# Sigmoids through ScalarE's exponential and logarithm, and the second layer's input weights held back until the expert rows are gathered

## The reference

```
h  = rms(x) * (1 + scale1) + shift1
p  = h @ w_in                         # (640, 2304)
pq, pk, pv, hq, hf_f, hf_b, hi, hg, pft = split(p)
# forget gates, forward and backward, z = hf_f or hf_b (256 columns each)
logf = log_sigmoid(z) + log1p(lb * exp(min(-z, 80)))
k    = (1 - lb) * sigmoid(-z)         # lb is 0 in layer 0
qh   = silu(hq)                       # 256 columns
o_h  = rms(gated_linear_recurrence(qh, k, hi, logf)) * silu(hg)   # hg: 256 columns
x = x + gate1 * (concat(attention, o_h, fourier) @ w_out)
x = x + gate2 * moe(h2)               # top-1 group, top-2 expert of 16 gated MLPs
```

## Time and profile before

| | |
|---|---|
| median of 3 executions | 1805.18 us (1804.99 to 1806.71) |
| the profiled execution's own time | 1805.76 us |
| its span | 1803.9 us |
| mean granted TensorE clock | 0.943 of full speed |
| busy: PE / DVE / ACT / POOL | 88% / 38% / 20% / 18% |
| DMA, mean over the span | 175 GB/s |

### The profile page before, as it was taken

One profiled execution on the slowest core, in us unless ns is written; L12 is line 12 of the kernel. 1 busy time (PEld: TensorE's weight loads), 2 busy tenths in 40 slices (PEclk: granted clock), 3 DMA queues, 4 the chain that ended last, 5 costly groups with the idle time before them and its releaser, 6 DMA issues.

```text
span 1803.9 us, 24901 instructions
## 1 busy us (share of the span) xinstructions
PE 1592.4 (88%) x10358; PEld 1159.0 (64%) x10358; DVE 686.0 (38%) x1230; ACT 369.0 (20%) x694; POOL 316.3 (18%) x305
## 2 busy tenths in 40 slices
PE   6999989777998999999969799988779859999995
PEld 5556567655555788888645556666555458888883
DVE  1284246666115122112156722757641332112224
ACT  2221246221003100000142111642200211000002
POOL 4000159332000000000100001964300010000002
PEclk9999999889998899999979899999879969999997
DMA  9921100422013999999942111013400069999985
GB/s 267 323 52 62 56 27 1 141 69 75 18 52 134 345 367 367 365 366 345 357 164 47 47 48 61 12 36 108 118 2 0 0 244 338 370 360 370 368 305 210
DMA packets 143496, 315.69 MB, mean 175 GB/s; under 512 B 25024, under 2 KB 99192, under 8 KB 130456
## 3 DMA queue, kind: packets, MB, share of 16 engines
q1 hardware_dynamic: 120240, 241.88, 39.5%
q0 software_dynamic: 11104, 37.26, 5.4%
q10 hardware_dynamic: 12040, 34.95, 4.9%
HBM read 279.46 MB, written 34.60 MB: 174 GB/s over the span
## 4 chain that ended last, share of the span: by engine, by line
PE 75%; DVE 11%; ACT 4%; DMA 4%; POOL 3%; issue 3%; ACTq 0%; POOLq 0%; DVEq 0%
PE ps L1764 20%; PE ps L1361 19%; PE ps L1778 10%; PE ps L1405 4%; PE ps L1601 3%; ACT scr L573 3%; PE ps L1481 3%; PE ps L1748 3%; POOL scr L504 2%; DVE scr L974 2%; PE ps L1661 2%; PE ps L1541 1%; PE ps L1504 1%; DMA pT<-h_rows,slot_tok 1%; DMA scr<-y_rows,slot_i 1%
## 5 line engine op out<-in xcount | busy, mean ns | idle before, releaser
L1764 PEld LDWEIGHTS ps<-hT,ring 128*128 128x128 f32 x3200 | 370.2, 194 | 26.6 <-issue 22.0
L1764 PE MATMUL ps<-hT,ring 128*128 128x128 f32 x3200 | 371.1, 277 | 3.4 <-ACT hT L573 3.4
L1361 PE MATMUL ps<-hT,ring 128*128 128x512 f32 x960 | 269.4, 442 | 19.6 <-DVE pT L1020 12.6
L1361 PEld LDWEIGHTS ps<-hT,ring 128*128 128x128 f32 x960 | 149.7, 195 | 141.7 <-issue 128.6
L1778 PE MATMUL ps<-ring,pT 128*128 128x512 f32 x400 | 179.6, 592 | 0.0
L545 POOL DMA_INDIRECT pT<-h_rows,slot_tok x50 | 47.2, 944 | 728.6 <-PE ps L1748 430.2
L573 ACT ACTIVATE pT<-ps 128x256 f32<-128x256 f32 (+3 forms) x74 | 33.4, 457 | 685.2 <-PE ps L1764 495.0
L1316 DVE TENSOR_TENSOR pT<-ps,pT 128x256 f32<-128x256 f32 x50 | 21.3, 425 | 328.5 <-ACT pT L573 328.5
L1361 PE MATMUL ps<-pT,ring 128*128 128x512 f32 (+1 forms) x512 | 139.0, 434 | 1.7 <-ACT pT L573 1.7
L504 POOL TENSOR_SCALAR scr<-scr,st 128x640 f32<-128x640 f32 (+1 forms) x80 | 128.7, 1627 | 43.4 <-DVE st L1029 43.3
L1778 PEld LDWEIGHTS ps<-ring,pT 128*128 128x128 f32 x400 | 72.3, 190 | 72.7 <-issue 72.7
(11 more groups left out here) (228 smaller groups left out, 1864.4 us busy)
## 6 DMA issues: line engine op xcount, KB each, us to landing
ring<-in_w_gate_dram SPq DMA_DIRECT2D x50, 1024.0 KB, 7.4
ring<-in_w_up_dram SPq DMA_DIRECT2D x50, 1024.0 KB, 7.7
ring<-in_w_down_dram SPq DMA_DIRECT2D x50, 1024.0 KB, 7.0
ring<-in_w_ada_dram SPq DMA_DIRECT2D x48, 1024.0 KB, 5.7
y_rows<-pT ACTq DMA_DIRECT2D x50, 512.0 KB, 8.1
ring<-in_w_in_dram SPq DMA_DIRECT2D x14, 1024.0 KB, 11.9
h_rows<-scr ACTq DMA_DIRECT2D x10, 512.0 KB, 2.6
ring<-in_w_in_dram SPq DMA_DIRECT2D x16, 256.0 KB, 4.5
```

The source lines that it names most:

```text
L1361: ins = mm(out[:, a:b], lhs, rhs[:, a:b], start=start, stop=stop, **kw)
L1764: last = mm(bank(2 + j, P, at + c * P), w[:, k, c * P:(c + 1) * P], xk[:, j, k, :], start=(k == 0), stop=(k == KC - 1))
```

## The change

Two independent edits. **The sigmoids.** For the gates, sigmoid(-z) = en / den is now computed as exp(min(-z, 0) - ln(den)): DVE subtracts the logarithm that is there anyway (semaphore `gt_d`), ACT exponentiates in place (`gt_k`), and DVE multiplies by `omlb` after the scan. For the SiLUs, ACT computes exp(-ln(1 + exp(-z))) in three steps, each waiting for the one before, and DVE keeps the last product alone. **The weights.** SP waits for all ten gathers of layer 0 before it issues the first `in` item of layer 1; everything behind it on SP waits with it.

```diff
@@ SP
                 elif kind == "in":
+                    if l > 0 and i == 0:
+                        for t in range(TT):
+                            sp.wait_ge(y_in[t], 32 * l)
@@ ACT gate
                 if l > 0:
                     A_(scr[:, 8, :], scr[:, 9, :], ACT.Ln).then_inc(gt_ln, 1)
+                act.wait_ge(gt_d, n + 1)
+                A_(scr[:, 10, :], scr[:, 10, :], ACT.Exp).then_inc(gt_k, 1)
@@ ACT silu
-                A_(scr[:, i % 2, :], pT[:, GATE_CHUNKS[i], :], ACT.Exp, scale=-1.0).then_inc(sl_e, 1)
+                e = scr[:, i % 2, :]
+                seq(A_(e, pT[:, GATE_CHUNKS[i], :], ACT.Exp, scale=-1.0))
+                seq(A_(e, e, ACT.Ln, bias=ones[:, 0:1]))
+                A_(e, e, ACT.Exp, scale=-1.0).then_inc(sl_e, 1)
@@ DVE silu
                 dve.wait_ge(sl_e, n + 1)
-                seq(V.tensor_scalar(e, e, 1.0, None, ALU.add))
-                seq(V.reciprocal(e, e))
                 V.tensor_tensor(pT[:, c, :], pT[:, c, :], e, ALU.mult).then_inc(sl_ok, 1)
@@ DVE gate
                 V.tensor_tensor(den, ep, en, ALU.add).then_inc(gt_den, 1)
-                dve.wait_ge(gt_den, n + 1)
-                seq(V.reciprocal(rden, den))
-                seq(V.scalar_tensor_tensor(decayed[:, i, :], en, omlb[:, l, i:i + 1], rden, ALU.mult, ALU.mult))
                 dve.wait_ge(gt_ln, n + 1 if l == 0 else 4 + 2 * (n + 1 - 4))
+                V.tensor_tensor(key, tn, lnden, ALU.subtract).then_inc(gt_d, 1)
+                dve.wait_ge(gt_d, n + 1)
...
                 V.tensor_tensor_scan(out=z[:, way], data0=K["restart"][:], data1=tn[:, way], initial=0.0,
-                                     op0=ALU.mult, op1=ALU.add).then_inc(gt_ok, 1)
+                                     op0=ALU.mult, op1=ALU.add)
+                dve.wait_ge(gt_k, n + 1)
+                V.tensor_scalar(decayed[:, i, :], key, omlb[:, l, i:i + 1], None, ALU.mult).then_inc(gt_ok, 1)
                 dve.wait_ge(gt_ok, n + 1)
```

More of the change, by code:

```diff
@@ L318, in build_program @@
         sl_e = sem("sl_e"); sl_ok = sem("sl_ok")
-        gt_in = sem("gt_in"); gt_e = sem("gt_e"); gt_den = sem("gt_den"); gt_ln = sem("gt_ln"); gt_ok = sem("gt_ok")
+        gt_in = sem("gt_in"); gt_e = sem("gt_e"); gt_den = sem("gt_den"); gt_ln = sem("gt_ln"); gt_ok = sem("gt_ok"); gt_d = sem("gt_d"); gt_k = sem("gt_k")
         dk_d = sem("dk_d"); dk_e = sem("dk_e"); dk_ok = sem("dk_ok")
@@ L964, in gate @@
                 ep, en, tp, tn = (scr[:, j, :] for j in (2, 3, 4, 5))
-                lnden, den, lnnum, num, rden = (scr[:, j, :] for j in (6, 7, 8, 9, 10))
+                lnden, den, lnnum, num, key = (scr[:, j, :] for j in (6, 7, 8, 9, 10))
                 evacuated(l, i)
```

## The result

| | median us | ratio to before | 95% interval |
|---|---|---|---|
| before | 1805.95 (4 runs, 1804.99 to 1808.70) | | |
| changed | 1788.12 (4 runs, 1787.74 to 1789.02) | 0.9891 | 0.9877 to 0.9905 |

The changed kernel is 17.8 us faster; 1786.2 was predicted, in a range of 1781.5 to 1791.8. The profiled execution took 1787.74 us with a span of 1785.9, 18.0 us less than that of before on both counts.

What follows compares the result with a forecast made beforehand. DVE's gates, delaying copies PE waits for, were taken as the path in layer 1, and gathers as the limit between layers. Gains of 1.8 + 12.2 + 5.0 = 19.0 us gave 1786.2 us, range 1781.5 to 1791.8.

Steps and rivals of the forecast that it cites:

- What bounds the kernel: Input projections: PE stood 12.6 us in three waits for DVE's copies of odd units, each behind two gates.
- The gates: On DVE, one gate falls from 10.59 to 7.6 us in layer 0 and from 12.89 to 10.5 in layer 1.
- the lower end taken: Gates' late product by `omlb` on DVE: taken as 0.49 us, with 0.89 as the upper bound.
- Layer 0: Input projection of layer 0: DVE now waits for PE, so PE's 1.82 us wait goes, 1.8 us gained.
- Layer 1: Input projection of layer 1: unit 7 starts 9.7 us earlier and the clock returns 2.5, together 12.2 us.
- The 2.5 us of the clock: Layer 1 from unit 7: with 1.1 us of wait left, 64 matmuls take 17.57 us instead of 20.09.
- The SiLUs: Both projections: ACT's extra steps and DVE's saved work are covered by PE's matmuls, so 0 us.
- The hold: Gathers between the layers: last weighing at 909.3 instead of 914.35, 5.0 us, all on the path.
- those bytes are modulation weights, issued before and not held: SP queue between 888 and 896 us: all 2.44 MB moved there were taken as modulation weights, outside the hold.
- the issue pace: POOL's gathers: last issue stays at 902.61, last weighing 6.39 us later, which gives 909.0.
- The rival in which this stretch shrinks: Between gathers and unit 0: PE's work gets closer together, clock stays up, 2.5 us more gained, 1783.7; chance 0.12.
- The rival of the longer gate: Layer 1: product at 0.89, unit 7 waits 2.7 us, 1787.8; if the clock also falls, 1790.3; chance 0.12.

Runs made afterwards that it cites:

- experiment 5: Changed kernel with the gates' last product as a two-tensor operation, ratio 0.9926; with the one-tensor product also done once more ahead of it, ratio 0.9927.
- experiment 3: Changed kernel with weights held until the root of layer 1's first norm, 1791.68 us, ratio 0.9919; or only until the first tile's gathers, ratio 0.9897.
- the second comparison: The changed kernel, not edited further, run once more against the kernel before: 1786.32 us, ratio 0.9897.
- experiment 4: Changed kernel with gate 3 behind unit 5, 1788.08 us; the same with ACT's squares of tiles 0 and 1 between its weighings, 1785.97 us.

## Why the prediction was right

- **What bounds the kernel.** Right: every wait named was DVE's copy behind two gates, and it went with them.
- **The gates.** Right in mechanism and nearly in size: 10.48 us for 10.5 in layer 1, and 7.63 (starts 85.56 and 93.19 in DVE's timeline) for 7.6 in layer 0. The product was 0.53 us, near the lower end taken (0.49), and with two tensors it was 0.86 in experiment 5. The Trainium skill (VectorE: DVE Perf Modes, "Mode 2x_2P") has a float32 operation on one tensor in SBUF run at twice the rate of one on two tensors; the trace agrees in direction for a per-partition scalar, though 0.86 is 1.6 times 0.53 and not twice.
- **Layer 0.** 1.8 us forecast; the wait of 1.82 is gone. The piece gained 2.25 between the two profiles, but it scatters by more than the difference, with the clock at unit 0's start: the hold alone, with the wait still there, took 80.20 us, less than the changed kernel's 80.64.
- **Layer 1.** 12.2 forecast, 11.45 measured (12.2 in the second profile of the changed kernel, 93.64 less 81.49; 12.2 with the gates alone, 93.64 less 81.48). The 0.7 us between the profiles of the changed kernel lie at the start of unit 0: the clock of its first 20 us read 0.88 in the first and 0.91 in the second, and seven units took 63.21 and 62.50 us. The wait left was 1.41 us, not 1.1. The 2.5 us of the clock came back in all five profiles with 1.41 or 1.42 us of wait (17.57 us for the 64 matmuls in each); with 2.73 us of it left, in experiment 5, 1.7 us stayed lost.
- **The SiLUs.** 0 forecast, 1.0003 measured.
- **The hold.** 5.0 forecast, 5.19 in the profile, 5.30 with the hold alone. The size came from the undisturbed gathers of layer 1 (17.68), beside 17.3 to 18.0 in the eight profiles in which the weights are held to the last gather or longer. One step of the account was wrong in part: "those bytes are modulation weights, issued before and not held". In the same window SP's queue moved 1.42 MB instead of 2.44, and the gathers 1.07 instead of 0.00. In the window that lies in the same place before and behind the first gather's issue, 887.1 to 895.1, SP's queue moved 1.68 MB and the gathers 0.72. So some 1.7 of the 2.44 MB may well have been modulation weights, and some 0.8 MB were held weights. The hold therefore also lets the gathers start sooner: the first weighing comes 7.03 us after the first issue instead of 9.39. It did not change the sum, since the end was taken from the issue pace. That pace was not quite right either: the last issue came 11.84 us after the first, not 11.19, and the last weighing 5.90 us after it, not 6.39. That the two nearly cancel is luck.
- **Not in the sum.** Last weighing to unit 0 was 22.97 to 23.14 us in the three profiles without a hold and 23.10 to 23.68 in seven with one and with ACT's squares where they were; the longer hold of experiment 3 stands apart. Its length goes with the clock: the four profiles at 22.97 to 23.14 us read 0.86 or 0.87 in it, the six at 23.67 or 23.68 us 0.79 to 0.84. Why six of the seven with a hold have the lower clock is open. The rival in which this stretch shrinks had it the wrong way round: the stretch grew by 0.1 to 0.7 us.
- **The total.** 19.0 forecast, 18.0 between the two profiles, 17.8 between the medians, and 21.0 in the second comparison (1807.33 less 1786.32). These lie no further apart than the recurrence's clock scatter. That the three forecast stages sum to 18.9 us in the first pair of profiles is partly luck: layer 0's 2.25 and layer 1's 11.45 both hold scatter of the clock at unit 0, in opposite directions, and the stages that were not in the sum came to -0.9 us together. The rival of the longer gate did not come true, but its second half was underrated: with 1.3 us more of wait the clock did fall in the one profile taken, for 1.7 us.

## What to carry to other kernels

When a serial chain on one engine feeds the copies out of PSUM that TensorE waits for, count the chain's operations one by one: here cheap operations on two engines in place of one dear one shortened each of layer 1's gates by 2.4 us and took 9.4 of the 10.8 us of waits away, and the same kind of replacement where TensorE covered it paid nothing. A shorter wait of TensorE can give back its clock as well: before units 5 and 7 it stayed up behind waits of 1.4 to 1.8 us and fell behind one of 2.7, so the step between was worth more than its length. At 2.7 us it is not certain to fall, as unit 0 of layer 0 shows. Prefetches that nobody needs yet should not share the transfer engines with a transfer on the path; hold them on a semaphore of the urgent one, and check that the time to their first use exceeds the landing time on an empty queue (here 23 us against 5 to 6).

## What the runs showed of the hardware that was not expected

- The granted clock behind a wait of TensorE before units 5 and 7: 17.57 us for 64 matmuls behind 1.41 to 1.82 us, 19.26 behind 2.73, 20.11 behind 5.10, 20.09 to 20.30 behind 9.13 (2.73 and 5.10 in one profile each). Behind the same 2.76 us before unit 0 of layer 0, seven units took 60.81 us in one profile and 63.49 and 63.57 in two others.
- Ten gathers of 0.5 MB needed 17.3 to 18.0 us from first issue to use whether or not some 0.9 MB of modulation weights still moved beside their start, against 20.5 with input weights from half way on and 22.9 to 23.0 with them from the start.
- A stage of 150 us with many short waits of TensorE varied by 4 us between executions (3 between the two of one kernel) with its granted clock, more than either small edit of experiment 4 gains.
